# First attention in head pairs: scores on the two partition halves, distance bias as two f32r products of a split strip, one strip load per head

## What is computed

```python
dist = BLOCK + i - j
band_ok = (dist >= 0) & (dist <= n_back)
bucket = t5_bucket(jnp.clip(dist, 0, n_back) * dil)
bias = jnp.transpose(bias_g[bucket].astype(jnp.float32), (2, 0, 1))
logits = einsum('znqhd,znkhd->znhqk', qb, kb) * (HEAD_DIM ** -0.5)
logits = jnp.where(mask, logits + bias, -jnp.inf)
...
wts = jax.nn.softmax(jnp.stack(lses, axis=0), axis=0)
attn = jnp.sum(wts[..., None] * jnp.stack(outs, axis=0), axis=0)
y_attn = (attn * jax.nn.silu(z_attn)) @ w_attn_br[l]
```

## Time and profile before

| | us |
|---|---|
| median of 3 executions | 1500.28 |
| lowest and highest | 1499.01, 1502.46 |
| the profiled execution | 1508.67 |
| its span, first to last instruction | 1507.0 |
| mean granted TensorE clock in it | 0.956 of full |
| TensorE busy in the span | 1376.6 (91%) |
| VectorE, ScalarE, POOL busy | 816.0, 598.1, 197.5 |

### The profile page before, as it was taken

The page is one execution under the profiler, slowest core; times in us unless marked ns, Lnnn a source line. Parts: engine busy times, 40 slices in busy tenths (PEclk is TensorE's granted clock), DMA queues, the critical chain, the costliest instruction groups (busy, mean ns, idle before and its releaser), DMA issues.

```text
span 1507.0 us, 25092 instructions
## 1 busy us (share of the span) xinstructions
PE 1376.6 (91%) x10449; PEld 1236.1 (82%) x10449; DVE 816.0 (54%) x1245; ACT 598.1 (40%) x955; POOL 197.5 (13%) x192
## 2 busy tenths in 40 slices
PE   5899999999999999888999999999997778789995
PEld 2799988789987778678889898998997557789995
DVE  1444434447543355547764555546667675566663
ACT  2443335343664344414421313223344773434440
POOL 1100101010001111115410000000030341200002
PEclk8899989999998999999999999999998998899998
DMA  8877754325245354325363434434224002255550
GB/s 316 283 245 241 245 172 141 124 96 192 91 139 157 127 193 142 112 91 162 112 206 117 153 113 157 149 112 144 100 93 140 1 1 85 70 182 180 183 195 28
DMA packets 159102, 218.19 MB, mean 145 GB/s; under 512 B 6126, under 2 KB 135541, under 8 KB 158878
## 3 DMA queue, kind: packets, MB, share of 16 engines
q1 hardware_dynamic: 141060, 152.30, 31.2%
q0 software_dynamic: 17248, 63.19, 12.3%
q10 hardware_dynamic: 698, 1.32, 0.3%
HBM read 215.70 MB, written 1.09 MB: 144 GB/s over the span
## 4 chain that ended last, share of the span: by engine, by line
PE 75%; DVE 12%; ACT 5%; DMA 3%; issue 3%; POOL 2%; SPq 1%; POOLq 0%; DVEq 0%; ACTq 0%
PE bank L1213 28%; PE bank L663 11%; PE bank L680 11%; PE bank L713 6%; PE bank L776 2%; DVE wlo L1913 2%; PE bank L696 2%; PE bank L891 2%; PE bank L889 2%; PE bank L1313 2%; DVE a_lo L2066 2%; DMA graw_b<-in_w_mod 1%; PE bank L1128 1%; PE bank L911 1%; PE bank L1057 1%
## 5 line engine op out<-in xcount | busy, mean ns | idle before, releaser
L1913 DVE TENSOR_TENSOR wlo<-raw,whi 128x2048 fp32r<-128x2048 f32 x77 | 175.6, 2282 | 113.6 <-ACT whi L1347 113.0
L1347 ACT ACTIVATE whi<-raw 128x2048 fp32r<-128x2048 f32 (+1 forms) x81 | 153.3, 1893 | 123.9 <-PE bank L1213 29.4
L1213 PE MATMUL bank<-whi,m_hi 128*128 128x256 f32 x640 | 181.8, 284 | 10.4 <-DVE m_lo L2427 7.5
L1213 PE MATMUL bank<-wlo,m_hi 128*128 128x256 f32 x640 | 180.6, 282 | 0.0
L1213 PE MATMUL bank<-whi,m_lo 128*128 128x256 f32 x640 | 180.4, 282 | 0.0
L2407 DVE TENSOR_TENSOR wlo<-raw,whi 128x2048 fp32r<-128x2048 f32 x53 | 121.5, 2292 | 53.6 <-ACT whi L1790 50.7
L1213 PE MATMUL bank<-a_lo,whi 128*128 128x256 f32 (+1 forms) x448 | 148.8, 332 | 0.0
L1213 PE MATMUL bank<-a_hi,wlo 128*128 128x256 f32 (+1 forms) x448 | 148.6, 332 | 0.0
L1213 PE MATMUL bank<-a_hi,whi 128*128 128x256 f32 (+1 forms) x448 | 148.5, 331 | 0.0
L1790 ACT ACTIVATE whi<-raw 128x2048 fp32r<-128x2048 f32 x50 | 95.4, 1907 | 128.4 <-PE bank L1213 128.2
L1213 PEld LDWEIGHTS bank<-whi,m_hi 128*128 128x128 f32 x640 | 122.1, 191 | 12.2 <-DVE m_lo L2427 8.7
(11 more groups left out here) (373 smaller groups left out, 3429.2 us busy)
## 6 DMA issues: line engine op xcount, KB each, us to landing
raw<-in_mlp_w SPq DMA_DIRECT2D x64, 1024.0 KB, 5.1
graw_b<-in_w_mod POOLq DMA_DIRECT2D x80, 512.0 KB, 4.8
raw<-in_w_in SPq DMA_DIRECT2D x32, 1024.0 KB, 5.8
raw<-in_ev_w_in SPq DMA_DIRECT2D x12, 1024.0 KB, 5.1
pre<-in_w_ada SPq DMA_DIRECT2D x16, 512.0 KB, 10.6
graw_a<-in_w_mod POOLq DMA_DIRECT2D x16, 512.0 KB, 4.5
strip<-distance_rows POOLq DMA_DIRECT2D x16, 384.0 KB, 3.7
raw<-in_od_w_qkv SPq DMA_DIRECT2D x6, 1024.0 KB, 4.9
```

Of the source, the lines that this page charges most:

```text
L1213: mm = nc.tensor.matmul(o, x, y, start=(k == 0 and i == 0), stop=(k == KT - 1 and i == 2))
L1347: nc.scalar.activation(whi[u % SPL][:, 0:kt * cols], raw[u % RAW][:, 0:kt * cols], ACT.Copy).then_inc(hi_done, 1)
L1913: nc.vector.tensor_tensor(wlo[s][:, 0:n], raw[u % RAW][:, 0:n], bf(whi[s], n), ALU.subtract).then_inc(lo_done, 1)
```

## The change

The steps are taken in pairs of heads: `steps` runs over the four pairs, and in a pair over the two query tiles. `logits(n)` issues the score products of the two heads in turn, each head into its own banks (2 and 3, 4 and 5), then for each head the bias as two products of `anti_r`, the anti-diagonal matrix in the f32r type, with the two parts of the strip. For W = 256 a part is one product of 512 columns (groups 0 and 1) and one of 256; for W = 128 it is one of 384. The line of distances is split at the start: its f32r value, and what that leaves. Both go to HBM (`distance_parts`) and come back in one load of 128 x 2 x 3 x 256 for a head, which serves both query tiles; there is one strip buffer for the even head and one for the odd, and a load waits until the pair before has used it. The odd head's buffer lies where the GEMV ring was, so its first load waits for quarter 39, and that quarter moves from behind unit 23 to behind unit 22. A whole unit (two halves) follows each pair step. Tiles 24 to 31 use banks 0 and 1 only. The maximum and the exponential of W = 128 take one instruction each in place of two.

```diff
-        strip = [sb(f"strip{i}", [P, GROUPS, 256], where=A) for i in range(2)]
-        prob = sb("prob", [P, 768], where=A)
+        strip = [sb("strip_a", [P, 2, GROUPS, 256], f32r, A), strip_b]
+        prob = [sb("prob0", [P, 768], where=A)]
...
-            line = sb("line", [HEADS, GROUPS, 384], where=e)
+            line = sb("line", [HEADS, 2, GROUPS, 384], f32r, e)
...
-        steps = [(qt, h) for qt in range(NT) for h in range(HEADS)]
-
-        def rounds(n):
-            return n if n < HEADS else HEADS + 2 * (n - HEADS)
+        steps = [(h2, qt) for h2 in range(HEADS // 2) for qt in range(NT)]
+        A_BANK = ((2, 3), (4, 5))
+
+        def rounds(n, e=0, j=0):
+            return 6 * (n // 2) + 2 * (n % 2) + e * (n % 2 + 1) + j
...
-            i = t % 4 if t < PAIR0 else (t - PAIR0) % 2 if t < PAIR1 else (t - PAIR1) % 4
+            i = t % 2 if 24 <= t < 32 or PAIR0 <= t < PAIR1 and PAIR0 % 2 == 0 else t % 4 if t < PAIR0 else (t - PAIR1) % 4
...
-            for n, (qt, h) in enumerate(steps):
-                if n >= 2:
-                    pool.wait_ge(at_s, n - 1)
-                pool.dma_start(strip[n % 2][:, :, :],
...
+            for h in range(HEADS):
+                h2, e = divmod(h, 2)
+                if h2:
+                    pool.wait_ge(at_s, 4 * h2 - 1 + e)
+                elif e:
+                    pool.wait_ge(gemv_done, Q_B)
+                pool.dma_start(strip[e][:, :, :, :],
+                               bass.AP(tensor=parts.tensor, offset=parts.offset + h * 2 * GROUPS * 384,
+                                       ap=[[1, P], [GROUPS * 384, 2], [384, GROUPS], [1, 256]])).then_inc(strip_full[e], 16)
...
-                quarters(1)
+                quarters(1 if u < 22 else 2 if u == 22 else 0)
...
+            pe.wait_ge(anti_done, 1)
+            def logits(n):
+                h2, qt = steps[n]
+                W = P * (qt + 1)
+                for e in range(2):
+                    if n:
+                        pe.wait_ge(at_p, 2 * n - 1 + e)
+                    pe.wait_ge(strip_full[e], 16 * (h2 + 1))
+                for g in range(GROUPS):
+                    for e in range(2):
+                        lane = slice(64 * e, 64 * e + 64)
+                        o = bank[A_BANK[e][1]][:, 0:W] if qt and g == 2 else bank[A_BANK[e][0]][:, g * W:(g + 1) * W]
+                        nc.tensor.matmul(o, qT[lane, g, h2, qt * P:(qt + 1) * P], kT[lane, g, h2, 0:W],
+                                         start=(g == 0 or qt * g == 2), stop=False, skip_group_check=True)
+                for e in range(2):
+                    for v in range(2):
+                        if qt:
+                            nc.tensor.matmul(bank[A_BANK[e][0]][:, :], anti_r[:, :],
+                                             strip[e][:, v, 0:2, :].rearrange("p g w -> p (g w)"),
+                                             start=False, stop=(v == 1), skip_group_check=True)
+                            mm = nc.tensor.matmul(bank[A_BANK[e][1]][:, 0:W], anti_r[:, :], strip[e][:, v, 2, :],
+                                                  start=False, stop=(v == 1), skip_group_check=True)
+                        else:
+                            mm = nc.tensor.matmul(bank[A_BANK[e][0]][:, 0:GROUPS * P].rearrange("p (g w) -> p g w", g=GROUPS),
+                                                  anti_r[:, :], strip[e][:, v, :, P:256],
+                                                  start=False, stop=(v == 1), skip_group_check=True)
+                    mm.then_inc(at_s, 1)
...
+            logits(0)
+            for n, (h2, qt) in enumerate(steps):
+                prob_transposes(n, 0, 0)
+                if n + 1 < len(steps):
+                    logits(n + 1)
+                if qt:
+                    prob_transposes(n, 0, 1)
+                    values(n, 0, 0)
+                    prob_transposes(n, 1, 0)
+                    values(n, 0, 1)
+                    prob_transposes(n, 1, 1)
+                    values(n, 1, 0)
+                    values(n, 1, 1)
+                else:
+                    prob_transposes(n, 1, 0)
+                    values(n, 0, 0)
+                    values(n, 1, 0)
+                col_unit(U_GATES + n, h_hi, h_lo, S, before[U_GATES + n])
...
             for g in range(GROUPS):
                 dve.wait_ge(line_mm, g + 1)
-                nc.vector.tensor_copy(line[:, g, :], bank[0][0:HEADS, 0:384]).then_inc(line_done, 1)
+                link(nc.vector.tensor_copy(line[:, 0, g, :], bank[0][0:HEADS, 0:384]))
+                nc.vector.tensor_tensor(line[:, 1, g, :], bank[0][0:HEADS, 0:384], line[:, 0, g, :].bitcast(f32),
+                                        ALU.subtract).then_inc(line_done, 1)
...
+            dve.wait_ge(load_k, 16)
+            nc.vector.tensor_copy(anti_r[:, :], anti).then_inc(anti_done, 1)
             take_mod(9)
```

More of the change, by code:

```diff
@@ L165, in build @@
         A = ExitStack()
-        graw_a = [sb(f"graw_a{i}", [P, 2, 512], where=A) for i in range(GSA)]
+        with ExitStack() as e:
+            graw_a = [sb(f"graw_a{i}", [P, 2, 512], where=e) for i in range(GSA)]
+        strip_b = sb("strip_b", [P, 2, GROUPS, 256], f32r, A)
+        sb("beside_strip", [P, GSA * 1024 - 2 * GROUPS * 256], where=A)
         sb("shift_h", [P, 16], where=A)
@@ L192, in build @@
         with ExitStack() as e:
[L193 removed]
+            sb("beside_line", [P, 1536], where=e)
             pre = [sb(f"pre{i}", [P, 2, 512], where=e) for i in range(GSP)]
@@ L198, in build @@
             vR = sb("vR", [P, GROUPS, NT, 512], where=e)
+            prob.append(sb("prob1", [P, 768], where=e))
+            anti_r = sb("anti_r", [P, P], f32r, e)
         with ExitStack() as e:
@@ L910, in values @@
                     g, kb = divmod(blk, qt + 1)
-                    mm = nc.tensor.matmul(bank[7][:, 384:384 + HD], probT[rc % 2][:, b, :], vR[:, g, kb, h * HD:(h + 1) * HD],
+                    mm = nc.tensor.matmul(bank[7][:, e * HD:(e + 1) * HD], probT[rc % 2][:, b, :], vR[:, g, kb, h * HD:(h + 1) * HD],
                                           start=(blk == 0), stop=(blk == 3 * (qt + 1) - 1), skip_group_check=True)
                 mm.then_inc(at_pv, 1)
[L915 to L924, removed]
-                if qt:
[L926 to L931, removed]
+            logits(0)
[3 more added lines that the diff above has]
+                    logits(n + 1)
+                if qt:
+                    prob_transposes(n, 0, 1)
[10 more added lines that the diff above has]
+                col_unit(U_GATES + n, h_hi, h_lo, S, before[U_GATES + n])
             pe.wait_ge(mz_part, 2)
             col_unit(32, mz_hi, mz_lo, S, before[32])
-            pe.wait_ge(at_z, len(steps))
+            pe.wait_ge(at_z, 2 * len(steps))
             for k in range(4):
@@ L1996, in _, with maximum @@
-            take_mod(9)
-            maximum(0)
-            for n, (qt, h) in enumerate(steps):
-                for j in range(qt + 1):
-                    rc = rounds(n) + j
-                    dve.wait_ge(at_t, rc + 1)
-                    if rc >= 2:
-                        dve.wait_ge(at_pv, rc - 1)
-                    nc.vector.tensor_copy(probT[rc % 2][:, 0:3, :], bank[6][:, 0:384].rearrange("p (b q) -> p b q", b=3))\
-                        .then_inc(at_pt, 1)
-                dve.wait_ge(at_p, n + 1)
-                link(nc.vector.tensor_tensor(stat[:, 14:15], stat[:, 12:13], stat[:, 13:14], ALU.add))
-                link(nc.vector.reciprocal(stat[:, 15:16], stat[:, 14:15]))
+            def maximum(n, e):
+                qt, c = steps[n][1], 8 + 8 * e
+                W = P * (qt + 1)
+                dve.wait_ge(at_s, 2 * n + e + 1)
+                last = nc.vector.tensor_reduce(stat[:, c:c + 1], bank[A_BANK[e][0]][:, 0:(3 - qt) * W], AX.X, ALU.max)
+                if qt:
+                    last = nc.vector.tensor_reduce(stat[:, c + 1:c + 2], bank[A_BANK[e][1]][:, 0:W], AX.X, ALU.max)
+                link(last)
+                nc.vector.tensor_scalar(stat[:, c + 2:c + 3], stat[:, c:c + 1], stat[:, c + qt:c + qt + 1], -1.0, ALU.max, ALU.mult)\
+                    .then_inc(at_mx, 1)
@@ new lines, in _ @@
+            dve.wait_ge(load_k, 16)
+            nc.vector.tensor_copy(anti_r[:, :], anti).then_inc(anti_done, 1)
+            take_mod(9)
+            maximum(0, 0)
+            maximum(0, 1)
+            for n, (h2, qt) in enumerate(steps):
+                for e in range(2):
+                    for j in range(qt + 1):
+                        rc = rounds(n, e, j)
+                        dve.wait_ge(at_t, rc + 1)
+                        if rc >= 2:
+                            dve.wait_ge(at_pv, rc - 1)
+                        nc.vector.tensor_copy(probT[rc % 2][:, 0:3, :], bank[6][:, 0:384].rearrange("p (b q) -> p b q", b=3))\
+                            .then_inc(at_pt, 1)
+                for e in range(2):
+                    c = 8 + 8 * e
```

(4 more changed lines are left out.)

88 lines of the change are left out of this document (39 added, 49 removed).

## The result

The changed kernel took 1478.88 us (median of 4 executions, 1471.57 to 1483.49) beside 1501.14 before (4 executions, 1499.01 to 1502.46): a ratio of 0.985, 95% interval 0.981 to 0.989, 22 us. Run again beside another 11 executions of the kernel before it was 0.978 (0.974 to 0.981), 35 us. The forecast of 1472 and 28 us lies between them. The two traces give 30 us: a span of 1476.9 against 1507.0.

A forecast was written before the change was run, and what follows sets the result against it. TensorE's issue was taken to bound the first attention stage. It falls from 127.2 to 97.7 us, 29.5 gained, less 1.5 at the start: 28 us off the 1500.28 median gives 1472 us, range 1463 to 1482.

The forecast's parts named there:

- The pair steps: First attention stage: eight pair steps replace sixteen head steps, 10.83 us for 128-wide and 11.77 for 256-wide, four of each 90.4.
- the low clock: Opening of the attention stage: the reduced TensorE clock goes on costing 4.4 us as today, bounds 0 and 6.
- the start: Start of the kernel: distance-line subtraction costs 0.6 us and writing 72 KB instead of 36 costs 0.9, together 1.5 lost.
- the alternating row: Trace row of 16 64-row, 128-wide instructions on alternating halves, 0.068 us each against 0.208 here; used to price the scores.
- halves not together: Rival for the score products: they stay at today's price, 16 us of the gain lost, 1488 us; chance 0.04.
- about 1.5 times for two row tiles: Estimate scaled from the page's 3.07 for four row tiles; scores would cost 2.5 and 1.7 us, gain 8 us smaller.
- 0.15 a pair step for all changes: Charge for TensorE switching between half-array and whole-array products: 0.15 us a pair step, bounds 0 and 0.3.
- A handoff: Bank 6 wait for the probT copy: 0.18 us open, three times in a 256-wide pair step, once in a 128-wide one.
- The term of zero: Strip loads of 768 KB per head, at 4.5 us each plus 1.5 of issue, arrive before the logits: cost 0.
- the lower bound: Start of the kernel, doubled line write: -0.5 us, because the later GEMV block finds the DMA engines freer.
- The rival with its 0.07: Clock kept: shorter gaps at the stage's opening leave the clock at full, 4.4 us more gained, 1468 us; chance 0.07.
- The slower rival: Clock falls in every pair step after the new handoffs; half of the stage low is +42, 1514 us; chance 0.02.

The follow-up runs named there:

- e2: Changed kernel with score products ordered three of head 0, then three of head 1, so adjacent ones share a half; 1478.55 us, stage 110.44.
- e3: Changed kernel with the bias as one 32-bit product in place of two f32r products, the strip's second part left out; 1480.40 us, stage 109.87.
- e5: Kernel before the change, with each head's score products grouped first and its 32-bit bias products after; 1495.77 us against 1503.60, ratio 0.994.
- e6: Changed kernel with the first half of weight unit 24 issued behind the first logits, ahead of the first transposes; 1477.54 us, stage 107.59.
- e7: Changed kernel with four weight-unit products before each wait for a probT copy, eight behind the last pair's first transposes; 1465.60 us, ratio 0.975.
- e8: Changed kernel with the slices of e7, the half unit of e6, and ScalarE reading the last GEMV sum before evacuating unit 23; 1466.48 us.

## Why the prediction was right, and for which reasons it was not

**The size was right, and where it comes from.** Between the opening and the last copies TensorE issues without a stop, before and after, and the forecast summed what it issues: 29.5 us, the moved quarter's 0.5 already taken off, against a measured 28.1 at the same clock from which the quarter's 0.6, ahead of the stage now, have still to come off: 27.5. The pair steps came to 11.00 and 12.28 us, forecast 10.83 and 11.77, which makes 2.7 us over the four pairs; that the sum is nearer than that is partly luck, since the low clock cost 3.5 instead of 4.4, and the start lost 0.5 instead of 1.5.

**The step that failed is the reason for the scores' price.** The prediction read the alternating row, 3.05 times as fast as today's products, as two halves running at once, and priced "halves not together" at 16 us. e2 took them apart and lost 3.6. The price of the earlier trace rows was a change between 64-row and 128-row products in front of every product, 0.2 us each, and the row I compared with had such a change only at its ends. The price came out right because the new scores stand in a group as that row does, not for the reason given: as to the mechanism this was luck. With e3 and e5 the parts can be told: in one pair (two heads, both widths) grouping takes the scores from 2.50 + 3.77 to 1.48 + 2.76 us (twelve instructions of 0.107 or 0.213, and 0.2 once), and the two halves take them on to 0.94 + 1.50; grouping takes the bias from 2.50 + 3.77 to 1.49 + 2.78, f32r from there to 0.90 + 1.60. Times four: 8.1 and 8.0 us for grouping, 7.2 for the halves, 7.1 for f32r, where e3 lost 6.5. The 1.48 + 2.76 are worked out, for in e2 the two heads still overlapped; so the split of the 15.3 us of the scores between grouping and halves is an estimate, of which e2 shows 3.6 for the strict alternation and e5 the price of a group. By it, about half of the 30.4 us that the logits lose (the handoffs take some of it back) is in the order of the products; e5 had some 10 us by that alone, in the old kernel with one head at a time.

Two readings of pages change with this. The page TensorEngine Tiling of the Trainium skill (Key Properties) says that changing the mode drains TensorE; I had let it change nothing in the sum, and it is the sentence that explains the old price best: e5 agrees, with 0.2 us a change. That it is merely the first load of other weights does not fit the rows: transposes right behind the bias take 0.33 for three, values right behind transposes 0.62 for six and the unit right behind values 5.71, with other weights each time and nothing on top. The 0.2 stands only where the rows change between 64 and 128. What happens in it, a drain or something else of the change, no run here shows. For the page TensorE: Matmul & The Clock Gate of the Trainium skill (Part 3) I had said that the trace disagrees with about 1.5 times for two row tiles, on the strength of 3.05; against grouped products of one half, as worked out above, the gain is 2.76 / 1.50 = 1.8 and 1.48 / 0.94 = 1.6, nearer to my 1.5 by the page than to 3.05, which had the changes in it.

**Terms mis-sized.** A 128-wide pair's bias took 0.90 for 0.70, its four 384-wide products being 0.16 each with 0.2 once; that is the fixed part again, of which I had charged 0.15 a pair step for all changes. A 256-wide pair's bias took 1.60 for 1.40 for the same reason, and the scores 0.94 for 0.82 and 1.50 for 1.44. A handoff costs 0.31 for 0.18: 0.12 of idling, and another 0.19 because the group behind the stop takes 0.52 instead of 0.33; 0.29 at the last of each step. Logits 0.57 and handoffs 0.48 more, less the 0.30 charged for changes and 0.10 in the unit, are the 0.7 us by which a pair is longer than forecast.

**Strips.** The term of zero held, the reason did not: I took 4.5 us of landing for 768 KB and it was 6.2 and 7.1, at most 7.4, so of 1.5 us or more of margin 0.1 was left: the forecast held by luck. The 5.1 us for 1024 KB that spoke for 4.5 are of a later stage; the units beside these strips land in 5.8 (median of `raw<-in_w_in` in the changed kernel). e6, e7 and e8 show the wait that stood behind it: 2.9, 0.7 and 3.6 us.

**Start.** The subtraction shows on the chain as its own 0.56 us, the write took 5.23 for 4.88, where I had charged 0.9. The quarter behind it ran at 52.54 for 52.02, half a microsecond of the 1.5 forecast. Part of the delay is given back by its block, which took 7.93 us for 8.69; that it finds freer DMA engines, as the lower bound had it, is likely but not shown. The moved quarter and this would make the 1.1 us by which unit 23 ends later in the first pair of traces; but unit 23 ends 3.6 us apart in two traces of the changed kernel, so that is not shown.

**Clock.** The rival with its 0.07 may have been priced too low: the full clock in the opening came in one of the changed kernel's two traces, and is worth 3.5 us, forecast 4.4. Its reason, shorter stops, is not what decides: with the same stops ahead of it the clock fell in one trace and not in the other. The slower rival (the clock falling in every pair step) did not come: the clock was 1.00 from the opening to 300 us in every trace, but for some 4 us behind the strip wait of e6.

## What to carry to other kernels

Before running small products side by side, group them by kind: in this kernel each change between 64-row and 128-row products cost 0.2 us, so three score and three bias products of 128 columns in alternation cost 2.50 us, and 1.73 in two groups (e5). When a rate is taken from another place of the trace, compare what stands around both rows, not the shapes alone. And when a load is hidden, write down by how much, since the next cover that shortens the time in front of it (e6 and e8) pays that difference back as a wait.

## What the runs showed of the hardware that I had not expected

- A group of 32-bit products costs 0.107 us for each 128 columns and instruction and 0.2 us once at its head (0.63, 1.06 and 1.49 us for two, four and six instructions of 256 columns). Weights loaded anew for each product inside a group cost nothing (e3).
- Score products of one half and then of the other overlap at the boundary: 2.03 us where twelve instructions one after the other, at 0.213 each, would take 2.56 (e2).
- The clock fell in the opening in some executions and not in others of the same kernel, with stops of the same length: 0.50 from 212 to 222 in one trace of the changed kernel, after stops of 1.16 and 0.32 us, and 1.00 all through in the other, with stops of 1.17, 0.32, 1.25 and 0.37. It stayed at full through a stop of 3.1 us in e8 and was low behind one of 2.9 in e6.
- 768 KB strips land little faster on SyncE's queue than on POOL's (5.6 and 6.9 us against 6.2 and 7.1 for the first and the second of two), and no faster as 32-bit floats than as f32r (6.3 and 7.3), while a 1024 KB weight unit of the same stage lands in 5.8.
